# Residual norms of a fused two-layer block: more weight units beside the norm, row statistics by column sums

## What is computed

```python
def rmsnorm(x, w):
    x32 = x.astype(jnp.float32)
    y = x32 * lax.rsqrt(jnp.mean(x32 * x32, axis=-1, keepdims=True) + RMS_EPS)
    return (y * w.astype(jnp.float32)).astype(x.dtype)

# layer 1
u = rmsnorm(h, norm_mix_pre_w); proj = u @ w_in            # attention + state space mixer
h = h + rmsnorm(mixed, norm_mix_post_w)                    # post1
f = rmsnorm(h, norm_ffn_pre_w)                             # fpre1
f = jnp.square(jax.nn.relu(f @ w_up)) @ w_down
h = h + rmsnorm(f, norm_ffn_post_w)                        # fpost1
# layer 2
h = rmsnorm_2(x, mix_pre_norm); u = h @ w_in_2             # pre2
y = jnp.concatenate([y_conv, y_ret], axis=-1) @ w_out_2    # 31-tap convolution | retention
x = x + rmsnorm_2(y, mix_post_norm)                        # post2
h = rmsnorm_2(x, ffn_pre_norm)                             # fpre2
f = (jax.nn.silu(h @ w_ffn_gate) * (h @ w_ffn_up)) @ w_ffn_down
x = x + rmsnorm_2(f, ffn_post_norm)                        # fpost2
e = jax.nn.sigmoid(x @ w_ple_gate) * (p @ w_ple_proj)
x = x + rmsnorm_2(e, ple_post_norm)                        # ple
```

## Time and profile before

| What | Value |
|---|---|
| median of 3 runs | 1890.59 us |
| profiled execution | 1892.49 us |
| its span | 1890.7 us |
| TensorE matmul busy | 1816.5 us (96%) |
| VectorE / ScalarE / GpSimd busy | 831.9 / 759.0 / 762.4 us |
| mean granted TensorE clock | 0.988 |
| share of TensorE in the chain that ended last | 90% |

### The profile page before, as it was taken

One profiled execution on the slowest core, in us unless ns is written; L12 is line 12 of the kernel. 1 busy time (PEld: TensorE's weight loads), 2 busy tenths in 40 slices (PEclk: granted clock), 3 DMA queues, 4 the chain that ended last, 5 costly groups with the idle time before them and its releaser, 6 DMA issues.

```text
span 1890.7 us, 23982 instructions
## 1 busy us (share of the span) xinstructions
PE 1816.5 (96%) x8460; PEld 1442.5 (76%) x8460; DVE 831.9 (44%) x1588; ACT 759.0 (40%) x1216; POOL 762.4 (40%) x586
## 2 busy tenths in 40 slices
PE   6999999999999999999999998999988999999987
PEld 4777788888888887678888885777765888888865
DVE  5554546667776112431212125897536333320053
ACT  4444554665555222341323233333343333332241
POOL 3322354333334454244444442533142444445442
PEclk9999999999999999999999999999989999999998
DMA  5222233333333322243332231321121323333311
GB/s 176 69 65 83 68 112 112 102 100 101 101 100 123 101 90 86 70 133 93 97 100 91 99 99 45 94 84 56 45 67 43 102 89 100 100 100 100 107 61 45
DMA packets 46641, 170.53 MB, mean 90 GB/s; under 512 B 5184, under 2 KB 5312, under 8 KB 46304
## 3 DMA queue, kind: packets, MB, share of 16 engines
q1 hardware_dynamic: 43776, 156.77, 26.8%
q10 hardware_dynamic: 2784, 12.65, 1.9%
HBM read 167.24 MB, written 2.16 MB: 90 GB/s over the span
## 4 chain that ended last, share of the span: by engine, by line
PE 90%; DVE 6%; issue 2%; ACT 1%; POOL 1%; DVEq 0%; POOLq 0%; ACTq 0%
PE bank L361 27%; PE bank L363 27%; PE bank L362 26%; DVE xs L1544 1%; PE bank L472 1%; PE bank L617 1%; PE bank L481 1%; PE bank L494 1%; DVE y_u L1547 1%; PE bank L621 1%; PE bank L601 1%; PE bank L740 1%; DVE u_lo L1912 0%; POOL w_lo L335 0%; PE bank L722 0%
## 5 line engine op out<-in xcount | busy, mean ns | idle before, releaser
L335 POOL TENSOR_TENSOR w_lo<-raw,w_hi 128x512 fp32r<-128x512 f32 x578 | 755.6, 1328 | 1095.8 <-ACT w_hi L893 1095.7
L361 PE MATMUL bank<-u_hi,w_hi 128*128 128x512 f32 x1528 | 611.6, 400 | 8.4 <-DVE u_lo L1912 2.6
L363 PE MATMUL bank<-u_hi,w_lo 128*128 128x512 f32 x1528 | 596.2, 390 | 0.0
L362 PE MATMUL bank<-u_lo,w_hi 128*128 128x512 f32 x1528 | 595.8, 390 | 0.0
L893 ACT ACTIVATE w_hi<-raw 128x1024 fp32r<-128x1024 f32 x289 | 304.1, 1053 | 284.9 <-PE bank L363 282.7
L361 PEld LDWEIGHTS bank<-u_hi,w_hi 128*128 128x128 f32 x1528 | 287.7, 188 | 76.7 <-issue 13.2
L363 PEld LDWEIGHTS bank<-u_hi,w_lo 128*128 128x128 f32 x1528 | 287.4, 188 | 61.7
L362 PEld LDWEIGHTS bank<-u_lo,w_hi 128*128 128x128 f32 x1528 | 287.9, 188 | 60.2 <-issue 3.1
L361 PE MATMUL bank<-v_hi,w_hi 128*128 128x512 f32 x320 | 128.1, 400 | 9.3 <-DVE v_lo L2081 8.4
L363 PE MATMUL bank<-v_hi,w_lo 128*128 128x512 f32 x320 | 126.5, 395 | 0.0
L362 PE MATMUL bank<-v_lo,w_hi 128*128 128x512 f32 x320 | 125.5, 392 | 0.0
(11 more groups left out here) (279 smaller groups left out, 2156.6 us busy)
## 6 DMA issues: line engine op xcount, KB each, us to landing
raw<-weights SPq DMA_DIRECT2D x289, 512.0 KB, 3.6
bc<-acs ACTq DMA_DIRECT2D x16, 512.0 KB, 3.9
xs<-x SPq DMA_DIRECT2D x4, 512.0 KB, 5.3
xs<-x ACTq DMA_DIRECT2D x1, 2048.0 KB, 8.1
out<-xs SPq DMA_DIRECT2D x8, 256.0 KB, 2.0
rt<-ret_tables ACTq DMA_DIRECT2D x1, 1536.0 KB, 6.0
dist<-att_tables SPq DMA_DIRECT2D x1, 512.0 KB, 10.7
p_raw<-p ACTq DMA_DIRECT2D x1, 512.0 KB, 6.9
```

What stands on the lines that cost most here:

```text
L335: return nc.gpsimd.tensor_tensor(w_lo[:, slot, w], raw[:, slot, w], w_hi[:, slot, w].bitcast(F32), ALU.subtract)
L361: mm(dst, w_hi[:, slot, w], hi, start=first, stop=False)
L362: mm(dst, w_hi[:, slot, w], lo, start=False, stop=False)
L363: return mm(dst, w_lo[:, slot, w], hi, start=False, stop=last)
```

## The change

- `stat_sum` becomes four matmuls with the squares as weights and a single column of ones; the sums come out one token per partition. `means` goes; one 128x4 instruction makes the variance. The factor takes fewer small steps, and `stat_broadcast` is four 128-column matmuls of a broadcast factor column with the identity. No 512-wide `diag` is written.
- `weighted_high`: ScalarE writes `u_hi` straight from `xs` with the weight as its scale; `u_lo` is one VectorE instruction from `xs`; `tmp` and L1908 go.
- `unit_triple` runs three units beside the chunks (banks 0, 1 and 5), `fourth_unit` the fourth in bank 4, ahead of `stat_broadcast`. The consumers of these four units read from those banks.
- Squares of `pre2` and `fpre2` are added in pairs on VectorE (`pair_add`) and summed by `stat_pair` before chunks 3, 5, 7 and after the triple. Squares of `fpre1` are taken in the first FFN turn, with one `stat_sum` behind it; so that turn stands apart from its loop on ScalarE and VectorE, as does the first `swiglu` turn.
- The scaling of the rotary tables moves behind twelve taps of the convolution, and `glu_scale(1)` ahead to behind two.

```diff
-            def unit_pair(turn, hi, lo, ready, ready0, beside=lambda c: None):
+            def unit_triple(turn, ready0, beside):
+                banks = (0, 1, THIRD)
+                for j in range(3):
+                    pe.wait_ge(lo_done, turn.unit(j) + 1)
...
+                for c in range(TILES):
+                    beside(c)
+                    pe.wait_ge(u_ready, ready0 + c + 1)
+                    for j in range(3):
+                        last_mm = exact(ps[banks[j]][:], turn.slot(j), c, u_hi[:, c, :], u_lo[:, c, :],
+                                        c == 0, c == TILES - 1)
...
+            def fourth_unit(turn):
+                pe.wait_ge(lo_done, turn.unit(3) + 1)
+                for c in range(TILES):
+                    last_mm = exact(ps[FOURTH][:], turn.slot(3), c, u_hi[:, c, :], u_lo[:, c, :], c == 0, c == TILES - 1)
...
-            def stat_chunk(q, c, n):
-                pe.wait_ge(sq_ready, q + 1)
-                mm(ms[:], ones, sq[:, c % 2, :], start=(c == 0), stop=(c == n - 1)).then_inc(sq_used, 1)
+            def stat_pair(name, n):
+                pe.wait_ge(sem("pair_added"), 4 * PAIRED[name] + n + 1)
+                for t in range(QB):
+                    last = mm(ms[:, t:t + 1], diag[:, t * P:(t + 1) * P], ones[:, 0:1], start=(n == 0 and t == 0),
+                              stop=(n == 3), skip_group_check=True)
...
-                mm(ms[:], ones, diag[:], start=True, stop=True).then_inc(sem("summed"), 1)
+                for t in range(QB):
+                    last = mm(ms[:, t:t + 1], diag[:, t * P:(t + 1) * P], ones[:, 0:1], start=True, stop=True)
...
-                mm(rb[:], ones, diag[:], start=True, stop=True).then_inc(rb_ready, 1)
+                for t in range(QB):
+                    last = mm(rb[:, t * P:(t + 1) * P], tiny[:, 40 + t:41 + t].broadcast_to([P, P]), ident,
+                              start=True, stop=True)
...
-            unit_pair(Turn("mix2"), u_hi, u_lo, u_ready, 16, early_stats("pre2"))
+            unit_triple(Turn("mix2"), 16, pairs_beside("pre2"))
+            stat_pair("pre2", 3)
+            fourth_unit(Turn("mix2"))
             stat_broadcast(STATS["pre2"][1])
...
+            def weighted_high(name, first_x, squares=True):
                 for c in range(C8):
                     act.wait_ge(x_ready, first_x + c + 1)
+                    af(u_hi[:, c, :], xs[:, c, :], ACT.Identity, scale=v(name, c)).then_inc(u_hi_ready, 1)
+                    if squares:
+                        square(q + c, c, xs[:, c, :])
...
                 def rest(c):
                     dve.wait_ge(u_hi_ready, n0 + c + 1)
-                    tt(u_lo[:, c, :], tmp[:, c % 2, :], u_hi[:, c, :].bitcast(F32), ALU.subtract)\
-                        .then_inc(u_ready, 1)
+                    stt(out=u_lo[:, c, :], in0=xs[:, c, :], scalar=v(name, c), in1=u_hi[:, c, :].bitcast(F32),
+                        op0=ALU.mult, op1=ALU.subtract).then_inc(u_ready, 1)
+                    if name in PAIRED and c % 2 == 0 and c:
+                        pair_add(c // 2 - 1)
...
                 for c in range(C8):
                     stt(out=y[:, c, :], in0=y[:, c, :], scalar=v(name, c), in1=rb[:], op0=ALU.mult, op1=ALU.mult)\
                         .then_inc(sem("y_scaled"), 1)
+                    if behind:
+                        if c:
+                            behind(c - 1)
+                        add(c)
```

More of the change, by code:

```diff
@@ L124 @@
     _q, _k = _q + max(1, _n) * _chunks, _k + _n
-SUMMED = {"pre1": 0, "post1": 1, "fpost1": 2, "post2": 3, "fpost2": 4, "ple": 5}
+SUMMED = {"pre1": 0, "post1": 1, "fpre1": 2, "fpost1": 3, "post2": 4, "fpost2": 5, "ple": 6}
+PAIRED = {"pre2": 0, "fpre2": 1}
+THIRD, FOURTH = 5, 4
 class Turn:
@@ L845, in _ @@
             keep_clock(3)
-            unit_pair(Turn("swiglu"), u_hi, u_lo, u_ready, 24, early_stats("fpre2"))
+            unit_triple(Turn("swiglu"), 24, pairs_beside("fpre2"))
+            stat_pair("fpre2", 3)
+            fourth_unit(Turn("swiglu"))
             stat_broadcast(STATS["fpre2"][1])
-            for j in range(2, 4):
-                unit(Turn("swiglu"), j, j % 2, j // 2, u_hi, u_lo)
             with pe.Fori(1, H2 // 2) as i:
@@ L1276, in _ @@
             stat_root(k)
-            squares_and_scaled("pre2", 8, 16)
+            weighted_high("pre2", 8)
             stat_root(STATS["pre2"][1])
@@ L1962, in ffn_turn @@
                     added(j)
-            with dve.Fori(0, 3) as i:
+            ffn_turn(0)
+            dve.wait_ge(sem("summed"), SUMMED["fpre1"] + 1)
+            ts(tiny[:, 56:60], ms[:, 0:QB], 1.0 / D, EPS, ALU.mult, ALU.add)
+            with dve.Fori(1, 3) as i:
                 ffn_turn(i)
@@ L2155, in _, with gated @@
             ret_rest(3)
-            post_norm("post2", y_u, after="swiglu", behind=scaling("fpre2", 16, 24))
+            post_norm("post2", y_u, after="swiglu", behind=scaling("fpre2", 24))
             keep_scale("fpre2", h_scale)
-            with dve.Fori(0, H2 // 2) as i:
+            def gated(i):
                 turn = Turn("swiglu", i)
                 for n in range(2):
+                    apart = isinstance(i, int) and n == 1
+                    gate, up = (THIRD, FOURTH) if apart else (0, 1)
                     ready(turn, 0, n)
-                    tt(sq[:, 0, :], ps[0][:], h_scale[:], ALU.mult).then_inc(out_free[0], 1)
+                    scaled = tt(sq[:, 0, :], ps[gate][:], h_scale[:], ALU.mult)
+                    if apart:
+                        scaled.then_inc(sem("apart_scaled"), 1)
+                    else:
+                        scaled.then_inc(out_free[0], 2 if isinstance(i, int) else 1)
                     dve.wait_ge(sem("gate2_tanh"), i * 2 + n + 1)
```

213 lines of the change are left out of this document (114 added, 99 removed).

## The result

| | median, us | runs | ratio to before, 95% interval |
|---|---|---|---|
| kernel before | 1890.55 | 6 | |
| changed kernel | 1897.57 | 6 | 1.0043 (1.0029 to 1.0057) |
| changed kernel, second series | 1896.97 | 8 | 1.0032 (1.0021 to 1.0042) |

The change makes the kernel 7.0 us slower by the medians (6 in the second series). The forecast was 1887.0, and its range ended at 1893.5. The profiled execution took 1895.6 us (span 1893.4), 3.1 more than that of before. It was the fastest of its six, so part of the loss does not show in it. TensorE's mean granted clock over the span is 0.980, before it was 0.988.

A forecast was written before the change was run, and what follows sets the result against it. TensorE, busy 96% of the span, was taken as the bound. Terms 4.1 + 6.5 + 6.4 - 6.6 - 6.8 = 3.6 us gained gave 1888.9 against the profiled execution, 1887.0 for the median; range 1878.5 to 1893.5.

The forecast's parts named there:

- Factors, 4.1: Post norms and ple: shorter chain sends the broadcast earlier, 1.2 us at three norms, 0.4 at fpost1, 0.1 at ple.
- first norm, 6.5: First norm: broadcast at about 16.4, not behind 21.67, and no clock fall; gain 6.5 us, bounds 4 and 7.5.
- The units: Three units beside the chunks and a fourth after: fpre1 gains 6.4 us, pre2 costs 6.6, fpre2 costs 6.8.
- fpre1, 6.4 won: First FFN norm: units start earlier, less a fourth-unit wait of 2.7 and clock loss; net gain 6.4 us, bounds 5 and 8.
- R: Time zero at each post norm: first use of its broadcast, 790.37 at post1, 1163.94 at fpost1, 1427.63 at post2.
- The chunk's loop: fpre1, per chunk: add, high half, low half take 2.02 us; TensorE needs 2.06 and is the bound.
- pre2, -6.6: mix2: fourth unit waits 4.25 us, x_scale 11 us late, 4.4 caught up; cost 6.6, bounds 3.3 and 11.
- Rival 2: Convolution stage: late x_scale not caught up, clock falls again behind glu_scale(2); 1896.2 us, chance 0.13.
- fpre2, -6.8: swiglu: unit 4's split stands behind the first tanh, which needs late h_scale; cost 6.8 us, bounds 2 and 9.
- rival 1: TensorE's clock holds, or falls for less, behind the new waits at fpre1, pre2, fpre2; 1878.6 us, chance 0.20.
- rival 3: First norm gives 4 us or less, since what follows is late or VectorE is held beside GpSimd; 1890.6, chance 0.11.
- rival 4: Low half of unit 3 is there in time at all three places; above 20 us gained, chance 0.02.

The follow-up runs named there:

- the two kernels with the factors alone: Kernel before plus only the change's shorter factor chain and broadcast from factors: with one-column sums 1888.18 us, with 512-column sums 1879.80 us.
- factors alone: Kernel before with only the change's one-column sums, shorter factor chain and broadcast straight from the factors: 1888.18 us (0.9994).
- the old sums: 512-column matmul and four multiply-reduces for the sums; put back at the post norms of the changed kernel 1887.60 us, kept in the kernel before with new factors 1879.80.
- second execution: The changed kernel run and profiled once more, unaltered: 1896.97 us.
- early splits: Changed kernel with the high half of unit 3, and of unit 4 in swiglu, earlier in ScalarE's list: 1883.71 us (0.9965).
- broadcast first: Changed kernel with the pre norm's broadcast ahead of the fourth unit in mix2 and swiglu: 1887.01 us (0.9991).
- taps: Changed kernel with glu_scale(2) four taps earlier in VectorE's list and the table scaling behind it: 1899.48 us (1.0038).
- the taps on the fastest: Fastest kernel with glu_scale(2) four taps earlier in VectorE's list and the table scaling behind it: 1868.09 us (0.9872).
- the fastest: Changed kernel with earlier high halves, 512-column post norm sums and the broadcast ahead of the fourth unit: 1864.25 us (0.9866).
- filler ahead: Changed kernel with one of the three fillers ahead of stat_sum at post1, fpost1, post2, fpost2 and ple: 1890.61 us (1.0009).

## Why the prediction was wrong

It forecast 3.6 us faster; the kernel is 7.0 slower, 10.6 us apart. The two kernels with the factors alone split that in two: 8.1 of the 10.6 lie in the factors and the first norm, 2.4 in the units.

**Factors, 4.1, and first norm, 6.5: the step that failed.** The step was "three fillers still stand between sum and broadcast, six passes of 0.43 us (about 2.6 us of the 2.74)" and "The fillers end at 16.87, a little earlier now". The part measured 10.5 us with the old sums, against 10.6 forecast, and 2.5 (by the ratio -0.6 to 2.8) with the sums that the change has. The shorter chain does what was worked out (sum to broadcast 3.54 with the old sums, 1.15 less than before, forecast 1.2). But the prediction took the one-column sums from the earlier trace rows by their duration alone, 0.95 us against 1.12, and did not ask what the clock does behind them. With the clock at half for a part or all of them, six filler passes take 4.1 to 5.5 us, and since the fillers set the broadcast, all of it is on the path. "Without the wait the clock should not fall" held: no trace with the factors has the fall of before at 21.1; the clock came up late instead. In the ledger the two kernels with the factors part by 4.9 us up to the sum of post1 (the first norm, and the falls near 94 and 224 us), 1.7 at post1, 1.4 at fpost1 and 1.7 at post2; 2.3 come back in the convolution stage and 1.6 in swiglu, where the slower one has fewer falls, and 1.4 are lost again behind fpost2. In the changed kernel the step from sum to broadcast of fpost1 took 6.9 us in the one execution and 3.57 in the other; forecast was 5.2 (0.4 less than the 5.65 of before).

**The units, -7.0 in all: nearly right.** The change against its factors alone is 9.4 us slower; with old sums in both it is 7.8 (1887.60 less 1879.80). The forecast was 7.0.

- *fpre1, 6.4 won.* From the first tile of fpre1 to the sum of fpost1 the change takes 356.7 us, before 360.8; with the 2.8 up to the first tile (R+3.16, forecast R+2.95, before R+5.98) 6.9. The wait before the fourth unit was 2.28 (forecast 2.7), with no fall in the first execution and one of 3.4 us in the second, which took 358.3 and so won 5.3. A cost of the squares in turn 0 does not show.
- *The chunk's loop* is 2.15 us, not 2.02, and VectorE sets the triple, not TensorE (2.06):

```profile
786.54 0.68 DVE L1581 TENSOR_TENSOR xs<-xs,y_u 128x512 f32<-128x512 f32 x1
...
787.25 0.73 ACT L1261 ACTIVATE u_hi<-xs,vec 128x512 fp32r<-128x512 f32 x1 [1.42 <-DVE xs L1581]
788.02 0.75 DVE L1955 SCALAR_TENSOR_TENSOR u_lo<-xs,vec,u_hi 128x512 fp32r<-128x512 f32 x1
788.68 0.69 DVE L1581 TENSOR_TENSOR xs<-xs,y_u 128x512 f32<-128x512 f32 x1
```

  ScalarE's high half takes 0.72 with a vector as scale, where the earlier trace rows had 0.61 without: 0.11 of the 0.13. The prediction had weighed against this the Trainium skill (VectorE: DVE Perf Modes, The DRAIN you can't avoid), by which the next instruction starts when the pipe is empty: 2.17. That number came out nearly, the reason did not: the low half (788.02 + 0.75) still overlaps the next add (788.68) by 0.09. The same section of the Trainium skill says that an instruction that is not held starts earlier, which the prediction had left out. The triple ended at R+20.4 (forecast R+19.4), 1.0 us late.
- *pre2, -6.6.* Wait 4.01 (forecast 4.25), fourth unit at R+27.7 (R+27.3), x_scale at R+36.8 (R+36.1), waits for `glu` of 1.44 and 4.67 (1.6 and 4). From the first tile to the first factor it is 119.3 against 108.1 us: 11.1 lost, less the 2.8 that the earlier first tile had won, 8.3; forecast 6.6 (7.8 in the second execution). The missing 1.7 fits the clock, though no run has it by itself: behind the wait of 4.67 too it was at half, for 4.1 us of work, about 2 us. Rival 2 had a fall there, but only where VectorE catches up less than 2 us; the factor of head 0 waited its old 2.50, so VectorE had caught up by then, on time that TensorE had lost.
- *fpre2, -6.8.* From R to the sum of fpost2 384.9 against 377.9 us: 7.0. Wait 6.32 (forecast about 6), unit 4 at R+43.1 (forecast R+42.3) and some 1.8 for the clock (2.4).

**Rivals.** The clock did not hold (rival 1). That rival had leaned on the 2.50 us wait before 1278.05 without a fall; in the same trace the clock was at 0.50 for 3.4 us behind each of the two later waits of 2.50 (1311.01 and 1349.00). Rival 2 was the right side, with the loss in pre2 somewhat above the forecast, but that its total of 1896.2 lies near the measured time is luck: it rests on terms that were not the cause. The first norm gave 5.8 and 4.8 us, more than rival 3's 4. Low halves were late (rival 4). Of GpSimd's share of the SBUF interfaces (GPSIMD Engine Reference, Specifications, in the Trainium skill) the changed kernel shows nothing at the first norm: its two scalings, each with one input in PSUM, took 1.41 together, as elsewhere, and its first subtraction started at 20.59, behind the end of the low halves (20.45). With the old sums, which bring the broadcast forward, the subtractions do wait, by 1.3 us: between the 0.5 of the prediction and the 2.5 that it had worked out by that rule. None of the rivals let a *new* fall happen at a norm whose wait stayed the same: that was the case left out.

## What to carry to other kernels

Fillers that keep a clock are part of the critical chain as soon as the chain beside them is shorter than they are: then put one into the wait ahead of the short work, not all behind it. (At the first norm this does not help: a filler stood ahead there in every kernel, and TensorE had not yet come up to full rate.) When a wide matmul is replaced by narrow ones of the same duration, look at what stands on both sides of it, and price everything up to the next full-width work at half rate as well. When units are pulled ahead of others, the high half of the first one that is no longer covered has to be pulled ahead on its own engine, and what releases the other engines (here the broadcast of the scale) goes ahead of work that nobody waits for: these two moves and the old sums turn 7.0 us lost into 26.4 won (1864.25 against 1890.66).

## What the runs showed of the hardware

**One-column matmuls behind 1.4 us of idle time can go with a fall of the clock.** At post1 and post2 the clock fell in each of the six traces that have one-column sums and nothing ahead of them there (changed kernel twice, early splits, broadcast first, taps, factors alone); in none with 512-column sums (before, three experiments with them and the taps on the fastest) or with a filler ahead (two). But at fpost2, with the same sum behind the same wait of 1.41, it held in four of the six and fell in two (early splits and broadcast first). The changed kernel and early splits:

```profile
1810.28 2.82 PE L430 MATMUL bank<-cst 128*128 128x512 f32 x6
...
1797.30 4.52 PE L430 MATMUL bank<-cst 128*128 128x512 f32 x6
```

At fpost1, with 2.18 us of idle time, it fell in three of the six, in before, and in two of the six others (one with a filler ahead, one with old sums). So the form of the sum decides at post1 and post2 and not everywhere; what else does, and what about the one-column matmuls it is, was not told apart.

**The falls near 94 and 224 us** are in six of the eight traces with one-column sums and in no trace with old sums at 94 (at 224 in before, at 221 in one). At 90 us VectorE shows a gap of its own (factors alone):

```profile
90.62 0.29 DVE L1648 SCALAR_TENSOR_TENSOR hd<-hd 128x128 f32<-128x128 f32 x1
91.36 0.66 DVE L1648 SCALAR_TENSOR_TENSOR hd<-hd 128x128 f32<-128x128 f32 x2 [0.45 <-issue]
```

TensorE waits 1.75 us there for `hd`, with the old sums 1.4. The gap of 0.42 to 0.45 us stands at the same instruction in every kernel with one-column sums, and at other places in those with old sums, which have more VectorE instructions ahead. What makes the gap no run shows. Nor does it make the falls by itself: the first execution of the changed kernel and the filler ahead have the gap and the wait of 1.7 us and no fall.

**Steps of VectorE beside GpSimd.** At the third factor of retention the changed kernel waits 3.96 us, before 2.51. The same kind of gap shifts two steps of VectorE into GpSimd's low half (1343.44 to 1345.92); before, it is one step. The changed kernel, then before:

```profile
1342.91 0.17 DVE L2083 RECIPROCAL tiny<-tiny 128x4 f32<-128x4 f32 x1
1343.51 1.21 DVE L2085 SCALAR_TENSOR_TENSOR tiny<-tiny 128x4 f32<-128x4 f32 x1 [0.43 <-issue]
1344.80 1.14 DVE L2087 TENSOR_TENSOR tiny<-tiny 128x4 f32<-128x4 f32 x1
...
1347.86 1.09 DVE L2047 SCALAR_TENSOR_TENSOR tiny<-tiny 128x4 f32<-128x4 f32 x1
```

Steps on four elements per partition that read two inputs from SBUF take 0.16 alone and 1.1 to 1.2 there, about the length of one of GpSimd's instructions (2.48 for two). The subtractions of the first norm took 1.68 and 1.00 in place of 0.68. So the rule of the Trainium skill (GPSIMD Engine Reference, Specifications), contention of an instruction with two SBUF inputs, does show here, and not in the scalings that read one input from PSUM.
